# A state-space layer in one fused kernel: where the head's step sizes live, who makes its first taps, and the order of its last products

## The chip, the cores and the metric

The kernel runs on one core of one Trainium2 chip. The metric is the device time of one execution in microseconds. A core has TensorE (PE, matrix products into the PSUM banks), VectorE (DVE), ScalarE (ACT), GpSimd (POOL) and SyncE (SP), whose queue here issues nearly all DMAs. Engines run their own instruction streams and meet at counting semaphores.

## The reference, cut to what matters

Four layers over 512 tokens of width 1024: a short convolution with a feed-forward part, a dilated attention with a feed-forward part, a state-space mixer (SSD) and a gated linear attention mixer. Only the third is touched:

```python
def ssd_mixer(u, ...):                                   # u: rmsnorm(h), 512 x 1024
    z, xbc, dt = split(u @ w_in, [2048, 2048 + 4096])     # dt: 64 = 2 directions x 32 heads
    xbc = silu(dwconv(xbc, conv_w, conv_b))               # 5 taps along the tokens, per channel
    dt = softplus(dt + dt_bias); a = -exp(a_log)
    y = ssd_scan(xh, dt[:, :, 0], a[0], B, C) + rev(ssd_scan(rev(xh), rev(dt[:, :, 1]), a[1], rev(B), rev(C)))
    y = (y + xh * d_skip) * silu(z)                       # then an rmsnorm per group of 256 channels
    return y @ w_out
def step(state, (x, dt, la, B, C)):                       # one chunk of 128 tokens, la = dt * a
    cum = cumsum(la); decay = exp(cum_l - cum_s) where s <= l
    y = (C B^T * decay) @ (x * dt) + (C @ state) * exp(cum)
    state = state * exp(cum_end) + B^T @ (x * dt * exp(cum_end - cum))
```

All is fp32 to the reader. A matrix product is made of three products of fp32r parts: high with high, high with low, low with high.

## The kernel before, in words

**Weights** come in units of 128 x 2048 elements. SP loads a unit into `raw[s]` (s is the unit's parity), ScalarE copies it to its high part `whi[s]` (`high`, L684, line 690), GpSimd subtracts to get the low part `wlo[s]` (`low`, line 612). `high(n)` waits until TensorE has marked unit n-2 as done (semaphore `mm`, two marks a unit), SP's load of unit n until the low part of unit n-2 is made, and TensorE's `unit(n)` until the low part of n is there. So three engines work a unit or two ahead of TensorE, and a unit of 48 products of 512 columns takes TensorE some 11 us.

**The state-space stage** has 8 groups of 4 heads. For group g TensorE projects two x tiles, B and C (`project`, q = 0 to 3, channels on partitions, 512 tokens along the bank) and z. VectorE's `taps(g, q)` (L1528) scales the bank by the norm, makes the middle tap with a tensor_scalar (line 1536) and adds the four others (line 1540); ScalarE applies silu (`silu`, L905). TensorE turns x and B to tokens (`turn_x`, `turn_bc`), makes the scores B C^T (line 2273), which VectorE masks (line 1551), the state increments (line 2285), and for each of 4 chunks the carried and the intra-chunk products (lines 2317, 2321). The decay exp(cum_l - cum_s) is made from rows of cum that SP spreads over the partitions from DRAM: ScalarE biases them (`biased`, line 956), VectorE takes a minimum (`least`, line 1566), ScalarE the exponential (line 973). SP fetches the rows of chunk n only when the exponential of chunk n-2 is done. VectorE's `states` (L1568) runs the recurrence over chunks, `collect` (L1583) adds up a chunk: the carried products times exp(cum), into `yt`, the intra-chunk part, and then `yt` itself. `gate` multiplies by silu(z); `normalise`, with squares and a root on ScalarE, is the group norm; TensorE turns the result (line 2299), ScalarE keeps it and makes its high part (`y_hi`), VectorE its low part (`y_low`, line 1610).

**The head** has more: TensorE projects x, B, C of group 0, the step sizes dt (64 rows, bank 4) and x of group 1 one after the other. VectorE brings dt to SBUF and ScalarE and VectorE make softplus, dt * a, the cumulative sums (two scans, line 1687), cum_end - cum (line 1690), its exponential and the product with dt (line 1694), between the taps of group 0, in the written order of each engine.

**The tail.** The last group is written out by hand (`last_group`, on each engine). The output product has 8 units (128 output channels, 16 blocks of 128 inputs). Blocks 0 to 13 of units 0 and 1 are multiplied in while the last group still runs; blocks 14 and 15 belong to the last group and come last. The other units follow in a loop: all of a unit waits for its low part. When a unit's last product is marked, VectorE adds it to the residual (line 1328), and ScalarE makes the next norm's high part and square (`split_square`) and, behind these in its order, the high part of the weight unit two further on.

The order of every engine's work is written out; there is no planner.

## Time and profile before

| | us |
|---|---|
| median of 3 runs (lowest, highest) | 2104.53 (2103.15, 2105.02) |
| the profiled execution | 2103.18 |
| its span | 2101.2 |
| state-space stage, first projection to the last output unit | about 1168 to 1668 |

The page gives for each engine the busy time and its share of the span. The views name a wait by who waited and by the instruction that ended last before it could go on. Times in a timeline are microseconds from the start of the span. The stages before and after the state-space one have the same code before and after.

### The profile page before, as it was taken

How to read it: one execution, taken by the hardware profiler on the slowest of the kernel's cores; microseconds unless marked ns; L12 is line 12 of the kernel's file. 1: busy time of each engine (PE TensorE's matmuls, PEld its weight loads, DVE VectorE, ACT ScalarE, POOL GpSimd, SP SyncE). 2: the span in 40 equal slices, each digit the busy share in tenths (PEclk: the TensorE clock that was granted, in tenths of full speed). 3: DMA queues.
4: the chain of work that ended last, by engine and by line, in shares of the span. 5: the costliest groups of instructions: out<-in, count | busy, mean ns of one | idle time of the engine just before them, and what ended most of it. 6: DMA issues, size and time to landing. Idle time of an engine off the chain costs nothing.

```text
span 2101.2 us, 27300 instructions
## 1 busy us (share of the span) xinstructions
PE 2039.3 (97%) x10588; PEld 1698.2 (81%) x10588; DVE 930.4 (44%) x1425; ACT 838.0 (40%) x1349; POOL 1043.2 (50%) x855
## 2 busy tenths in 40 slices
PE   8999999999999999999999979999988999999998
PEld 6878888888777777888888768888976878888886
DVE  3184433421244443333313588888882224434231
ACT  4123222222344443222223467776772235553442
POOL 4445554545523324554455468888873432323342
PEclk9999999999999999999999989999998999999999
DMA  4223233323432213233233243443422331111231
GB/s 161 86 98 111 81 100 100 94 83 97 118 111 81 71 61 99 83 100 100 82 97 103 76 133 101 117 125 104 132 84 63 91 94 61 60 62 62 58 83 60
DMA packets 267034, 193.37 MB, mean 92 GB/s; under 512 B 9443, under 2 KB 263703, under 8 KB 266920
## 3 DMA queue, kind: packets, MB, share of 16 engines
q1 hardware_dynamic: 264380, 191.20, 30.6%
q8 instruction: 82, 1.34, 0.3%
q10 hardware_dynamic: 2540, 0.56, 0.1%
q14 instruction: 32, 0.26, 0.0%
HBM read 189.46 MB, written 2.27 MB: 91 GB/s over the span
## 4 chain that ended last, share of the span: by engine, by line
PE 54%; issue 24%; POOL 15%; DVE 4%; ACT 2%; DMA 0%; POOLq 0%; ACTq 0%; SPq 0%; DVEq 0%
PE bank L1895 16%; PE bank L1896 15%; PE bank L1897 15%; POOL wlo L612 15%; PE bank L2321 1%; PE bank L2504 1%; PE bank L2317 1%; PE bank L2285 1%; DVE xc L1540 1%; PE bank L2520 1%; ACT whi L690 0%; PE bank L2518 0%; PE bank L2478 0%; PE bank L2465 0%; DVE kg L1756 0%
## 5 line engine op out<-in xcount | busy, mean ns | idle before, releaser
L612 POOL TENSOR_TENSOR wlo<-raw,whi 128x512 fp32r<-128x512 f32 (+1 forms) x668 | 855.3, 1311 | 983.4 <-ACT whi L690 983.4
L1895 PE MATMUL bank<-hHi,whi 128*128 128x512 f32 x1408 | 557.1, 396 | 8.3 <-DVE xc L1540 2.9
L1897 PE MATMUL bank<-hHi,wlo 128*128 128x512 f32 x1408 | 549.1, 390 | 0.0
L1896 PE MATMUL bank<-hLo,whi 128*128 128x512 f32 x1408 | 548.8, 390 | 0.0
L690 ACT ACTIVATE whi<-raw 128x2048 fp32r<-128x2048 f32 (+1 forms) x168 | 303.7, 1808 | 456.3 <-PE bank L1897 451.7
L1895 PEld LDWEIGHTS bank<-hHi,whi 128*128 128x128 f32 x1408 | 264.8, 188 | 69.4 <-issue 8.5
L1897 PEld LDWEIGHTS bank<-hHi,wlo 128*128 128x128 f32 x1408 | 264.6, 188 | 56.2
L1896 PEld LDWEIGHTS bank<-hLo,whi 128*128 128x128 f32 x1408 | 264.9, 188 | 54.4 <-issue 1.2
L1895 PE MATMUL bank<-whi,hHi 128*128 128x256 f32 x896 | 262.8, 293 | 4.8 <-ACT gO L1205 3.7
L1897 PE MATMUL bank<-whi,hLo 128*128 128x256 f32 x896 | 253.4, 283 | 0.0
L1896 PE MATMUL bank<-wlo,hHi 128*128 128x256 f32 x896 | 253.3, 283 | 0.0
L1895 PEld LDWEIGHTS bank<-whi,hHi 128*128 128x128 f32 x896 | 171.6, 191 | 15.1 <-issue 14.7
L1896 PEld LDWEIGHTS bank<-wlo,hHi 128*128 128x128 f32 x896 | 171.6, 192 | 3.7 <-issue 3.7
L1328 DVE TENSOR_TENSOR xT<-xT,bank 128x512 f32<-128x512 f32 x48 | 33.0, 687 | 317.8 <-PE bank L1897 316.2
L1897 PEld LDWEIGHTS bank<-whi,hLo 128*128 128x128 f32 x896 | 171.5, 191 | 0.0
L1540 DVE SCALAR_TENSOR_TENSOR xc<-bank,vecT,xc 128x510 f32<-128x510 f32 (+1 forms) x96 | 72.0, 750 | 3.4
L1897 PE MATMUL bank<-f0aHi,wlo 128*128 128x512 f32 x176 | 68.5, 389 | 0.0
L1897 PE MATMUL bank<-f1aHi,wlo 128*128 128x512 f32 x176 | 68.5, 389 | 0.0
L1895 PE MATMUL bank<-f0aHi,whi 128*128 128x512 f32 x176 | 68.5, 389 | 0.0
L1896 PE MATMUL bank<-f0aLo,whi 128*128 128x512 f32 x176 | 68.5, 389 | 0.0
L1895 PE MATMUL bank<-f1aHi,whi 128*128 128x512 f32 x176 | 68.5, 389 | 0.0
L1896 PE MATMUL bank<-f1aLo,whi 128*128 128x512 f32 x176 | 68.5, 389 | 0.0
(340 smaller groups left out, 2923.3 us busy)
## 6 DMA issues: line engine op xcount, KB each, us to landing
raw<-in_ssd_w_in SPq DMA_DIRECT2D x48, 512.0 KB, 4.9
raw<-in_ffn_w_gate SPq DMA_DIRECT2D x44, 512.0 KB, 4.7
raw<-in_ffn_w_up SPq DMA_DIRECT2D x44, 512.0 KB, 4.6
raw<-in_gla_w_in SPq DMA_DIRECT2D x40, 512.0 KB, 4.5
rows<-cums SPq DMA_DIRECT2D x64, 256.0 KB, 5.5
raw<-in_conv_w_in SPq DMA_DIRECT2D x24, 512.0 KB, 4.4
raw<-in_ffn_w_down SPq DMA_DIRECT2D x32, 384.0 KB, 3.5
raw<-in_attn_w_qkv SPq DMA_DIRECT2D x24, 512.0 KB, 4.3
```

What stands on the lines that cost most here:

```text
L612: ins = pool.tensor_tensor(wlo[s][:, part], raw[s][:, part], whi[s][:, part].bitcast(F32), ALU.subtract)
L690: act.activation(whi[s][:, 0:w], raw[s][:, 0:w], ACT.Copy).then_inc(w_hi, 1)
L1328: tt(x, x, bank[b][:, :], ALU.add).then_inc(res_done, 1)
L1540: ins = stt3(y[:, to:to + w], u[:, frm:frm + w], tapcol(j, ct), y[:, to:to + w], ALU.mult, ALU.add)
L1895: pe.matmul(dst, hi1, hi2, start=first, stop=False)
L1896: pe.matmul(dst, hi1, lo2, start=False, stop=False)
L1897: return pe.matmul(dst, lo1, hi2, start=False, stop=last)
L2285: ins = pe.matmul(bank[4 + step][:, 256 * d:256 * d + 256], bt[:, P * c:P * (c + 1)], xw_buf(step, d), start=True, stop=True)
L2317: pe.matmul(carried_bank(c, d), conv_tile(g, 3)[:, P * c:P * (c + 1)], m["stt"][:, SEQ * step + 256 * d:SEQ * step + 256 * d + 256], start ...
L2321: ins = pe.matmul(intra_bank(c)[:, 64 * h:64 * h + 64], weights(n)[:, P * h:P * (h + 1)], xt[:, 256 * c + 64 * h:256 * c + 64 * h + 64], s ...
L2504: pe.matmul(bank[4 + 2 * d + n % 2][:, :], tile(t32[d], t, P), values(h, t), start=True, stop=True).then_inc(S("gu_mm"), 1)
L2520: ins = pe.matmul(out[:, :], decayed_q(h, d)[:, P * t:P * (t + 1)], state(d, t), start=n >= 2, stop=True)
```

## The change

Six edits:

1. Taps of group 0: VectorE scales the bank (`tap_scale`), ScalarE makes the middle tap out of the bank (`tap_mid`), VectorE adds the other four (`tap_rest`), with the four tiles interleaved. Groups 1 to 7 stay as they are.
2. The step sizes stay in PSUM bank 4 (`dt4`) through softplus and the later product; ScalarE makes a copy in SBUF for TensorE's transposes.
3. The end decays exp(cum_end - cum) are 8 ScalarE activations with scale -1 and a bias, one for each direction and chunk, in place of two VectorE subtractions and one exponential.
4. TensorE turns step sizes, sums and decays first and x of group 0 after them; ScalarE copies them in that order too.
5. `collect` writes the scaled carried product back to its bank and adds from there; `yt` goes, and the bank is released after the last add.
6. The last group on VectorE: `states` before the second `least`, `normalise` after two low parts; on TensorE: the last turn before the low parts of unit 1, unit 0 finished before unit 1's low weights, and unit 2 written out: 32 products with the high weights, which wait for the high part alone, then 16 with the low weights.

```diff
-                  ("stt", [P, 3 * SEQ], F32), ("xC1", V, F32), ("xt", [P, NT * 256], F32), ("MT", [P, 3 * SEQ], F32), ("yt", V, F32),
+                  ("stt", [P, 3 * SEQ], F32), ("xC1", V, F32), ("xt", [P, NT * 256], F32), ("MT", [P, 3 * SEQ], F32),
...
+    def tap_mid(g, q):
+
+        ct = 2 * g + q if q < 2 else (16 if q == 2 else 24) + g
+        act.wait_ge(S("tap_scaled"), 4 * g + q + 1)
+        act.activation(conv_tile(g, q), in_bank(g, q)[:, :], ACT.Copy, scale=tapcol(2, ct)).then_inc(S("tap_mid"), 1)
...
-    dtT, tmp, cum, wsT = headed("MT", 0), headed("MT", 1), headed("stt", 0), headed("stt", 2)
-    chain(act.activation(tmp, dtT, ACT.Abs, bias=hcol[:, 0:1]))
+    dt4, tmp, cum, wsT = bank[4][0:DTH, :], headed("MT", 1), headed("stt", 0), headed("stt", 2)
+    chain(act.activation(tmp, dt4, ACT.Abs, bias=hcol[:, 0:1]))
     chain(act.activation(tmp, tmp, ACT.Exp, scale=-1.0))
+    tap_mid(0, 0)
     act.activation(tmp, tmp, ACT.Ln, bias=1.0).then_inc(S("dt_log"), 1)
     unit_high(UNIT_OF["x", 1])
+    tap_mid(0, 1)
...
+    act.wait_ge(S("la_made"), 1)
+    copy(headed("MT", 0), dt4, S("dt_kept"))
     for q in range(2):
         silu(0, q)
+    tap_mid(0, 2)
     unit_high(UNIT_OF["bc", 1])
     act.wait_ge(S("cum_ready"), 1)
     for d in range(2):
         act.activation(dirs_of(m["hcol"][:, 4:8])[d].unsqueeze(2), last_of(cum, d), ACT.Exp).then_inc(S("decay_exp"), 1)
-    act.wait_ge(S("ws_diff"), 2)
-    act.activation(wsT, wsT, ACT.Exp).then_inc(S("decay_exp"), 1)
+    for d in range(2):
+        for c in range(NT):
+            ins = act.activation(v3(dirs_of(wsT)[d], NT)[:, c, :], v3(dirs_of(cum)[d], NT)[:, c, :], ACT.Exp, scale=-1.0,
+                                 bias=last_of(cum, d)[:, c, :])
+    ins.then_inc(S("decay_exp"), 1)
+    tap_mid(0, 3)
...
-    for b in range(2):
-        token_copy(0, b)
...
         copy(to, frm[:, ::-1, :] if d else frm, S("decay_kept"))
+    for b in range(2):
+        token_copy(0, b)
     silu(0, 2)
...
-    tt(dtT, bank[4][0:DTH, :], rstd[0:DTH, :], ALU.mult).then_inc(S("dt_pre"), 1)
+    dt4 = bank[4][0:DTH, :]
+    tt(dt4, dt4, rstd[0:DTH, :], ALU.mult).then_inc(S("dt_pre"), 1)
...
         chain(tt(u[:, :], u[:, :], rstd[:, :], ALU.mult))
         chain(ts(y, u[:, :], tapcol(2, ct), None, ALU.mult))
+        taps_beside(g, q)
+
+    def taps_beside(g, q):
+
+        ct = 2 * g + q if q < 2 else (16 if q == 2 else 24) + g
...
         ins.then_inc(S("tap_done"), 1)
+
+    def tap_scale(g, q):
+
+        dve.wait_ge(mm, 2 * UNIT_OF["x" if q < 2 else "bc", g] + q % 2 + 1)
+        u = in_bank(g, q)
+        tt(u[:, :], u[:, :], rstd[:, :], ALU.mult).then_inc(S("tap_scaled"), 1)
+
+    def tap_rest(g, q):
+
+        dve.wait_ge(S("tap_mid"), 4 * g + q + 1)
+        taps_beside(g, q)
...
-        y, yt = chunk("ybuf", c), m["yt"]
...
+        y = chunk("ybuf", c)
...
         dirs = [d for d in range(2) if not (c == 0 and d == 0) and not (c == 3 and d == 1)]
         if len(dirs) == 2:
-            chain.note(tt(dh(yt[:, :]), dh(bank[(5, 7)[c - 1]][:, :]), heads2("ecum", c, g), ALU.mult))
+            carried = bank[(5, 7)[c - 1]][:, :]
+            chain.note(tt(dh(carried), dh(carried), heads2("ecum", c, g), ALU.mult))
         else:
-            d = dirs[0]
-            chain.note(tt(h4(yt[:, 256 * d:256 * d + 256]), h4(carried_bank(c, d)), bc(heads("ecum", c, d, g), 64), ALU.mult))
+            carried = carried_bank(c, dirs[0])
+            chain.note(tt(h4(carried), h4(carried), bc(heads("ecum", c, dirs[0], g), 64), ALU.mult))
         chain(tt(y, y, intra_bank(c), ALU.add))
+        for n in range(len(dirs)):
+            chain(tt(y, y, carried[:, 256 * n:256 * n + 256], ALU.add))
         dve.sem_inc(S("y_bank_free"), 1)
-        for d in dirs:
-            chain(tt(y, y, yt[:, 256 * d:256 * d + 256], ALU.add))
...
         normalise(g - 1)
         least(n)
         low(U_SSD_OUT)
+        states(g)
         least(n + 1)
-        states(g)
         y_low(0)
         least(n + 2)
         for k in range(1, 3):
@@ -1638,10 +1671,10 @@
         collect(g, 2)
         collect(g, 3)
         gate(g, 1)
-        for k in range(5, 10):
+        for k in range(5, 7):
             y_low(k)
         normalise(g)
-        for k in range(10, IT):
+        for k in range(7, IT):
             y_low(k)
...
-    taps(0, 0)
+    tap_scale(0, 0)
+    tap_scale(0, 1)
+    tap_rest(0, 0)
     dve.wait_ge(S("dt_log"), 1)
-    chain(ts(dtT, dtT, hcol[:, 0:1], 0.0, ALU.add, ALU.max))
-    chain(tt(dtT, dtT, tmp, ALU.add))
+    chain(ts(dt4, dt4, hcol[:, 0:1], 0.0, ALU.add, ALU.max))
+    tt(dt4, dt4, tmp, ALU.add).then_inc(S("dt_made"), 1)
+    dve.wait_ge(S("dt_made"), 1)
     dve.wait_ge(S("decay_exp"), 1)
-    chain(ts(laT, dtT, hcol[:, 1:2], -1.0, ALU.mult, ALU.mult))
-    taps(0, 1)
+    ts(laT, dt4, hcol[:, 1:2], -1.0, ALU.mult, ALU.mult).then_inc(S("la_made"), 1)
+    dve.wait_ge(S("la_made"), 1)
+    tap_rest(0, 1)
+    tap_scale(0, 2)
     for d in range(2):
         way = slice(None, None, -1 if d else 1)
         chain(dve.tensor_tensor_scan(dirs_of(cum)[d][:, way], dirs_of(again)[d], dirs_of(laT)[d][:, way], 0.0, ALU.mult, ALU.add))
     dve.sem_inc(S("cum_ready"), 1)
-    for d in range(2):
-        tt(v3(dirs_of(wsT)[d], NT), last_of(cum, d).broadcast_to([SSD_HEADS, NT, P]), v3(dirs_of(cum)[d], NT), ALU.subtract).then_inc(S("ws_diff"), 1)
+    tap_scale(0, 3)
+    tap_rest(0, 2)
     dve.wait_ge(S("decay_exp"), 3)
     tt(v3(m["back"][0:DTH, 0:256], NT), rep(ident[0:DTH, 0:DTH], NT), bc(m["hcol"][0:DTH, 4:8], DTH), ALU.mult).then_inc(S("et_spread"), 1)
     dve.wait_ge(S("decay_exp"), 4)
-    tt(wsT, wsT, dtT, ALU.mult).then_inc(S("ws_made"), 1)
-    for q in range(2, 4):
-        taps(0, q)
+    tt(wsT, wsT, dt4, ALU.mult).then_inc(S("ws_made"), 1)
+    tap_rest(0, 3)
...
-            pe.wait_ge(S("dt_pre"), 1)
+            pe.wait_ge(S("dt_kept"), 1)
+            pe.wait_ge(S("ws_made"), 1)
...
         out_high(1, range(14))
-        out_low(1, range(14))
         for e in range(2):
             turn_out(g, e)
-        unit(U_SSD_OUT + 1)
-        out_low_weight(1, range(14))
+        out_low(1, range(14))
         for k in range(2):
+            if k:
+                unit(U_SSD_OUT + 1)
+                out_low_weight(1, range(14))
             for j in range(14, IT):
                 out_high(k, (j,))
                 out_low_weight(k, (j,))
                 mark(out_low(k, (j,)))
 
-    turn_x(0)
     pe.wait_ge(S("cum_ready"), 1)
+    pe.wait_ge(S("dt_kept"), 1)
...
+    turn_x(0)
...
-    for k in range(2, KT):
+    pe.wait_ge(w_hi, U_SSD_OUT + 3)
+    for j in range(IT):
+        w = slice(P * j, P * (j + 1))
+        pe.matmul(out_bank(2)[:, :], whi[0][:, w], tile(sHi, j), start=j == 0, stop=False)
+        pe.matmul(out_bank(2)[:, :], whi[0][:, w], tile(sLo, j), start=False, stop=False)
+    unit(U_SSD_OUT + 2)
+    for j in range(IT):
+        ins = pe.matmul(out_bank(2)[:, :], wlo[0][:, P * j:P * (j + 1)], tile(sHi, j), start=False, stop=j == IT - 1)
+        if j >= IT - 2:
+            mark(ins)
+    for k in range(3, KT):
```

## Rows read from the trace of the kernel before

**Rows 1.** The page's first part: engine, busy us (share of the span), instructions.

```profile
PE 2039.3 (97%) x10588; PEld 1698.2 (81%) x10588; DVE 930.4 (44%) x1425; ACT 838.0 (40%) x1349; POOL 1043.2 (50%) x855
```

**Rows 2.** TensorE's waits, whole span: waited for; us in total, times, longest.

```profile
PE bank L1895 <- POOL wlo L612: 11.8, 4, 8.5
...
PE bank L2317 <- DVE stt L1580: 5.5, 2, 3.3
...
PE bank L2273 <- ACT xC L908: 3.1, 1, 3.1
PE bank L2266 <- ACT xc L908: 2.9, 1, 2.9
PE bank L1895 <- DVE xc L1540: 2.9, 1, 2.9
```

**Rows 3.** Two stretches: busy us of each engine, granted clock, DMA share, GB/s.

```profile
1280.00:1325.00 45.00, 45.00 (x277) 40.24 (x276) 38.97 (x56) 31.42 (x69) 38.51 (x34) 1.00 0.44 118
1601.00:1605.00 4.00, 3.28 (x9) 2.61 (x10) 0.00 (x0) 0.00 (x0) 4.00 (x4) 0.55 0.48 138
```

**Rows 4.** Timeline of VectorE, head: start, us, line, operation, tile, count, idle before.

```profile
1191.67 0.47 DVE L1680 TENSOR_SCALAR MT<-MT,hcol 64x512 f32<-64x512 f32 x1
1192.17 1.66 DVE L1681 TENSOR_TENSOR MT<-MT 64x512 f32<-64x512 f32 x1
...
1202.45 2.38 DVE L1690 TENSOR_TENSOR stt<-stt 32x512 f32<-32x512 f32 x2 [0.15 <-DVE stt L1687]
...
1213.92 3.10 DVE L1540 SCALAR_TENSOR_TENSOR xC<-bank,vecT,xC 128x510 f32<-128x510 f32 x4
...
1217.66 0.75 DVE L1536 TENSOR_SCALAR xc<-bank,vecT 128x512 f32<-128x512 f32 x1
...
1221.47 0.68 DVE L1551 TENSOR_TENSOR CB<-bank,LE 128x512 f32<-128x512 f32 x1
```

**Rows 5.** Groups of instructions by line: count, busy us, mean ns, idle before.

```profile
L1599 DVE TENSOR_TENSOR ybuf<-ybuf,yt 128x256 f32<-128x256 f32 x48 | 42.7, 889 | 5.5 <-DVE ybuf L1596 4.9
...
L1596 DVE TENSOR_TENSOR ybuf<-ybuf,bank 128x256 f32<-128x256 f32 x32 | 13.1, 409 | 0.0
...
L956 ACT ACTIVATE rows<-rows,ncum 128x128 f32<-128x128 f32 x128 | 40.7, 392 | 8.5 <-DMA rows<-cums 8.3
...
L999 ACT ACTIVATE sY<-bank,vecT 128x512 f32<-128x512 f32 x16 | 10.7, 671 | 12.2 <-PE bank L2299 12.2
```

**Rows 6.** Timeline of TensorE, head.

```profile
1208.74 1.03 PE L2257 MATMUL bank<-ident,xc 128*128 128x128 f32 x8
...
1217.83 2.08 PE L2273 MATMUL bank<-xC,xc 128*128 128x128 f32 x8 [3.11 <-ACT xC L908]
```

**Rows 7.** Timeline of ScalarE, head.

```profile
1209.38 1.08 ACT L710 ACTIVATE xt<-bank 128x512 f32<-128x512 f32 x2 [3.88 <-PE bank L2257]
...
1213.23 0.72 ACT L908 ACTIVATE xc<-xc,vecT 128x512 f32<-128x512 f32 x1
```

**Rows 8.** Timelines of the last group and the tail: VectorE, TensorE, ScalarE, GpSimd.

```profile
1540.72 2.67 DVE L1617 TENSOR_TENSOR wlo<-raw,whi 128x2048 fp32r<-128x2048 f32 x1 [1.33 <-ACT whi L690]
1547.01 0.70 DVE L1566 TENSOR_TENSOR bank<-bank,rows 128x512 f32<-128x512 f32 x1 [3.61 <-ACT bank L956]
...
1592.00 0.69 DVE L1328 TENSOR_TENSOR xT<-xT,bank 128x512 f32<-128x512 f32 x1 [1.68 <-PE bank L2361]
...
1561.25 1.13 PE L2317 MATMUL bank<-stt,xC 128*128 128x256 f32 x4 [1.93 <-ACT szs L981]
...
1587.10 3.43 PE L2355 MATMUL bank<-sHi,wlo 128*128 128x512 f32 x14
...
1601.72 0.80 PE L1895 MATMUL bank<-sHi,whi 128*128 128x512 f32 x1 [8.47 <-POOL wlo L612]
...
1593.87 1.89 ACT L690 ACTIVATE whi<-raw 128x2048 fp32r<-128x2048 f32 x1
...
1595.84 10.78 POOL L612 TENSOR_TENSOR wlo<-raw,whi 128x512 fp32r<-128x512 f32 x8 [24.42 <-ACT whi L690]
```

More of the change, by code:

```diff
@@ L1521, in _ @@
                 dve.wait_ge(S("rstd_ready"), MID + 1)
-                dtT, tmp, laT, cum, wsT = headed("MT", 0), headed("MT", 1), headed("MT", 2), headed("stt", 0), headed("stt", 2)
+                tmp, laT, cum, wsT = headed("MT", 1), headed("MT", 2), headed("stt", 0), headed("stt", 2)
                 hcol = m["hcol"][0:DTH, :]
-                tt(dtT, bank[4][0:DTH, :], rstd[0:DTH, :], ALU.mult).then_inc(S("dt_pre"), 1)
+                dt4 = bank[4][0:DTH, :]
+                tt(dt4, dt4, rstd[0:DTH, :], ALU.mult).then_inc(S("dt_pre"), 1)
                 dve.wait_ge(S("spread"), MID + 1)
@@ L1531, in taps @@
                     y = conv_tile(g, q)
-                    n = 4 * g + q
                     dve.wait_ge(mm, 2 * UNIT_OF["x" if q < 2 else "bc", g] + q % 2 + 1)
@@ L1536, in taps @@
                     chain(ts(y, u[:, :], tapcol(2, ct), None, ALU.mult))
+                    taps_beside(g, q)
+                def taps_beside(g, q):
+                    ct = 2 * g + q if q < 2 else (16 if q == 2 else 24) + g
+                    y, u = conv_tile(g, q), in_bank(g, q)
                     for j in (0, 1, 3, 4):
```

## The prediction

> **What bounds the kernel now.** The page first: TensorE is busy for 97% of the span [rows 1], so an edit on another engine can pay only where TensorE stands idle, or runs at the lower clock after it has. The next view, what TensorE waited for over the whole execution [rows 2], names those places. One wait of 8.5 us for a low weight half made on GpSimd is the largest in the kernel; it lies at the end of the state-space stage. The head of that stage has four: 3.1 and 2.9 us for a ScalarE silu, 2.2 us (with the 3.3 us of the last group in one row) for the states, 2.9 us for VectorE's taps. In the last group TensorE also waits 1.9 us for the silu of z [rows 8]. The stretches [rows 3] show the rest: in a middle group TensorE is busy for 45.00 of 45 us, so whatever VectorE saves there is hidden, and after the long wait the granted clock is 0.55, near the lower of the two levels.
>
> All of the change therefore has to be read at two places, 1185 to 1240 us and 1545 to 1605 us. At the head VectorE works almost without a break from 1186 us on: it ends tap (0,3) at 1217.0 (its row starts at 1213.92 and takes 3.1), tap (1,0) at 1221.5, and then masks the scores [rows 4].
>
> **Head: taps and decays.** Each of the four tiles loses one VectorE tensor_scalar (0.78 us with its gap) to ScalarE, where the nearest row is a scaled copy out of PSUM, 671 ns [rows 5]; VectorE gains 3.1 us. The step sizes stay in bank 4. The SBUF-with-SBUF add took 1.66 us beside GpSimd's weight halves [rows 4]; with one operand in PSUM the adds of this kernel take 0.69 at 512 columns, as the first mask row does with 0.68. That is 1.0 us, and I take as much again for the last product, which has the same form. The two subtractions for the end decays (2.38 us in all, same form [rows 4]) go away. Against it stand the first tensor_scalar, which alone took 0.47 us and with PSUM takes 0.75, and nothing else on VectorE. Sum for VectorE: 3.1 + 1.0 + 1.0 + 2.4 + 0.4 (the product with a_log, which also sat beside GpSimd) - 0.3 = 7.6 us earlier at the end of tap (0,3), at about 1209.4.
>
> One rule speaks against the move to PSUM. The 0.47 us row is an SBUF tensor_scalar, the 0.75 us row one from PSUM [rows 4]. The Trainium skill (VectorE: DVE Perf Modes, "Why PSUM operands drop a tier") says that a PSUM operand costs such an instruction its double rate, and the trace agrees. By that rule alone two tensor_scalars would lose 0.3 us each; the row with GpSimd at work gives the second one back, as it was slowed more than that.
>
> ScalarE takes on 8 exponentials in place of 1: pieces of 128 columns start 0.31 us apart (392 ns each in the row, with overlap) [rows 5], 2.5 us for 0.6; four middle taps, 2.7 us; and one copy of the step sizes, 0.6. It stood idle for 3.9 us before 1209.38 [rows 7] and for longer before silu (0,1), which holds all of it, except that the first middle tap stands ahead of the high weight half of the next x unit. That moves this half by 0.65 us; its low half on GpSimd then no longer runs beside VectorE's slow add, and I cost this at nothing (if not, TensorE waits 0.65 us longer for that unit).
>
> Not all of the 7.6 us arrives. TensorE reaches its transposes at 1208.74 whatever VectorE does [rows 6]: its projections fill the time until then. Then comes a chain that the change leaves as long as it is: small transposes (1.4 us, now ahead of turn_x), five ScalarE copies and two token copies (2.6 from the first to the table load), the load (1.28) and silu (0,2) (0.72): it ends at 1214.0, where before it ended at 1213.95 [rows 7]. TensorE's turn of it and the copy take until 1215.4, silu (0,3) until 1216.1. Only this last one waited for VectorE, whose tap ended at 1217.0, and TensorE's scores came at 1217.83 [rows 6]. Scores now start at 1216.1 and, at the lower clock as before, are there about 2 us later. VectorE has done tap (1,0) by 1215.7 and waits; the first mask starts at 1218.2 against 1221.47, that is 3.3 us earlier. Everything behind it (least, exponential, row DMAs, states, chunk 0, tap (1,1)) keeps its distance, so project (1,3), which starts at 1236.03 when tap (1,1) has ended (the 2.9 us wait), starts at 1232.7. From there TensorE was full. **Head: -3.3 us**, bounds -1 (the ScalarE chain eats most) and -5.8 (1221.5 less 1215.7, if it were VectorE alone).
>
> **Collects.** 48 adds of 889 ns (SBUF with SBUF, beside GpSimd) become adds of 409 ns from PSUM [rows 5]: 23 us of VectorE work, of it some 20 in middle groups, hidden under a full TensorE. The bank is released after the last add, 0.9 us later; the next x transposes that wait for it came 5.6 us after the old release at group 0. Nothing for both. In the last group the collects end about 2 us sooner, which the next part uses up.
>
> **Last group: states ahead of the second minimum.** states starts at 1543.4, when VectorE has made its weight half, not behind the second minimum at 1547.6 [rows 8], and so ends about 4 us sooner, at 1548.0 by its five pieces (4.6 us). TensorE's 3.3 us wait goes. But the second minimum, at 1547.01, slips by 1.0 us. The exponential, the DMA of the last decay rows, their biases, the last exponential and silu z follow one after another, and TensorE's wait for z moves from 1561.25 [rows 8] to 1562.25 and grows from 1.9 to some 7.5 us. The wait of 1.9 us left the clock alone, that of 8.5 us did not: in the 4 us behind it 9 matmuls start at a clock of 0.55, 0.43 us apart, where 14 at the full clock take 3.43 us [rows 3, 8], 1.3 us lost. I expect the same here. (The Trainium skill, TensorE: Matmul & The Clock Gate, Part 1, says the throttled state is the default and activity releases it; these rows agree, and by the row alone the loss is the same.) So 2.3 us are lost there and the 2 us from collects come back. normalise now stands after two low parts instead of five. VectorE's total is unchanged and ScalarE's root covers itself as before, so the 14th low part still comes when it did, and TensorE waits as long for the parts, only elsewhere. Net +0.4, bounds -2 and +2.
>
> **Tail: output unit 2.** The last matmul of units 0 and 1 starts at 1592.86 and the next at 1601.72, 8.47 us of idle time [rows 8]. In between: the first residual (1592.00), ScalarE's split and square, the high half (1593.87, 1.89 us), GpSimd's low half (5.4 of the 10.78 us for two). The new loop needs only the high half for its first 32 matmuls, 32 x 0.227 = 7.3 us, which covers the 5.4. And the turns and unit 0's end now come before unit 1's 14 low-weight products (3.43 us at 1587.10) and 6 others (1.4). From the first residual, which follows unit 0's last matmul by 0.5 us, to the end of the high half are 1595.76 - 1592.00 = 3.8 us, so 4.3 in all; TensorE has 4.8 us of work. So the gap closes, with 0.5 us to spare: -8.5. The clock isn't lost either: -1.3. Of what moves: unit 0's end now stands behind the same four ScalarE and two VectorE pieces (4.0 us from the first turn) with 14 low products (3.2) and the turns (0.8) as cover: nothing. GpSimd makes the halves of units 2 and 3 back to back, 10.8 us from the end of the high half; TensorE wants unit 3 after 0.5 + 10.9: it just fits. SP's loads of units 2 and 3 wait for halves of units 0 and 1 alone, which GpSimd ended 24 us before its next work, and are long there. **Tail: -9.8 + 0.4 = -9.4 us**, bounds -12 and -6.
>
> **Sum.** -3.3 - 9.4 = -12.7 us. Against the profiled execution (2103.18 us, span 2101.2) that is 2090.5; the median of the runs, 2104.53, stands 1.35 above it, and the prediction goes by it: 2091.8. Changes within 0.2% (4 us) can't be told from none here.
>
> **Rivals.** (a) Only the tail pays: ScalarE, with the added pieces between, brings silu (0,2) and (0,3) no earlier. For it: the chain above has no slack to 1214.0. Against: 9 us of idle time on ScalarE. 2104.5 - 9.4 = 2095.1. (b) Both in full: the scores come when VectorE is ready, z is not later and the collects' 2 us count: -5.8 - 9.8 - 2.0 = -17.6, 2086.9. Against: the rows DMA follows the exponential. (c) Unit 2 doesn't close the gap: if ScalarE's order or the load holds back the high half as long as before, only the low half (5.4 us) is covered; 2104.5 - 3.3 - 5.4 = 2095.8, or 2099 with the head lost as well. (d) Slower: the collects now write their product back into its bank and read it there once or twice more, while TensorE fills others; no row shows a head-broadcast product from PSUM into PSUM. If they held the banks longer, TensorE would stall at the x transposes in each of 7 groups. The release has 5.6 us of room, of which 0.9 is used; the kernel is slower than before only if each release comes 4.7 + 12.7/7 = 6.5 us later still. VectorE has only 6 us of idle time per group, so that would cost as much: at 7.5 us later, 7 x 2.8 - 12.7 = +7, 2111.
>
> **Chances.** Forecast 60%, (a) 13%, (b) 10%, (c) 12%, (d) 2%, nothing or less by other causes 3%. Faster by over 0.2%: 93%; within: 4%; slower: 3%. The range takes in (a), (b) nearly, and (c): 2086.5 to 2098.
>
> **What would show it.** Head: "TensorE waits for ScalarE xC" at about 1216, the first mask at 1218.2, project (1,3) at 1232.7; VectorE idle before the mask by 2 to 3 us (it had none). Middle groups: TensorE still 45 of 45, VectorE's adds at 0.41. Last group: no wait for the states, one of about 7 us for silu z, then 0.5 of the clock. Tail: no wait of over 1 us between the last matmul of unit 1 and unit 2. It is wrong if the wait for z is short, if the gap before unit 2 stays, or if a middle group is longer than 45 us.

## The result, and the profile after

The kernel after takes **2090.97 us** (median of 5 runs, 2089.01 to 2092.32), the kernel before on the same chip 2103.15 (5 runs, 2101.06 to 2105.02): 12.2 us less. The ratio is 0.9939, 95% interval 0.9926 to 0.9951; by the ratio it is 12.8 us less, with an interval of 10.3 to 15.6. Forecast were 2091.8 us and -12.7, counted from the median of 2104.53 that was known then. The profiled execution took 2089.12 us (span 2087.4), against 2103.18 (2101.2) before.

To read where the time went, the span is cut at four instructions that every version has: the first scale of the step sizes on VectorE, the start of project(1, 3) on TensorE, VectorE's first mask of the last group, and the first residual of output unit 2 (the third `xT<-xT,bank` of 128x512). Times in us, each from one profiled execution:

```
kernel                                 first cut   head  middle  last group+tail   rest    span
before                                   1185.94  50.09  298.83      79.40       486.94  2101.2
after                                    1183.23  46.82  298.91      71.45       486.99  2087.4
the tail edit alone                      1186.09  50.10  299.14      69.44       486.93  2091.7
after, states behind the least gates     1184.60  47.27  299.34      69.15       487.04  2087.4
after, TensorE's wait for z filled       1185.86  47.27  298.78      69.48       487.11  2088.5
after, unit 2 as before                  1183.63  47.31  298.85      79.01       487.00  2095.8
after, taps on VectorE                   1183.67  46.54  299.16      71.70       488.33  2089.4
after, step sizes in SBUF                1186.36  47.29  300.02      70.27       486.96  2090.9
after, silu table early                  1184.17  44.46  299.08      71.42       486.97  2086.1
after, collects through SBUF             1185.69  46.81  298.87      72.13       487.00  2090.5
after, table early + states behind       1185.72  44.71  299.71      69.39       486.97  2086.5
the same, wait filled                    1184.20  45.86  299.47      69.26       487.01  2085.8
after, again                             1183.13  47.26  298.79      71.51       486.91  2087.6
```

The pair of executions differs by 13.8 us: 3.3 in the head, 8.0 in the last group and tail, nothing in the middle, and 2.7 ahead of the first cut, where both kernels are the same. That last part is a difference between executions (the column holds 1183.1 to 1186.4 for kernels that don't differ there). 1.6 us of it arise at one place: behind a wait of 1.8 us that both kernels have, the granted clock from 794 to 798 us is 0.80 in before and 1.00 in after. So the change is worth 11.2 us by the two stretches of the pair, 12.2 by the medians and 12.8 by the ratio. Where the code of a stretch is the same, the column scatters too: by 0.5 us in the head (by 1.4 in the three kernels with the early table), 1.2 in the middle and 1.4 in the last stretch; single numbers are read with that in mind. The rest column holds 486.9 to 487.1 but for one execution of 488.33; there the granted clock is 0.61 from 1708 to 1712 us, where the kernel after has 1.00.

The page's first part answers to [rows 1]. VectorE has lost 34 us, of which the kernel got little: TensorE is what counts.

```profile
PE 2035.4 (98%) x10588; PEld 1695.2 (81%) x10588; DVE 896.1 (43%) x1419; ACT 843.0 (40%) x1361; POOL 1034.3 (50%) x855
```

What TensorE waited for, whole span, against [rows 2]:

```profile
PE bank L2355 <- ACT szs L996: 6.3, 1, 6.3
...
PE bank L1932 <- POOL wlo L612: 3.3, 3, 1.8
PE bank L1932 <- DVE xc L1561: 3.1, 1, 3.1
PE bank L2304 <- ACT xc L908: 2.9, 1, 2.9
...
PE bank L2399 <- DVE sLo L1643: 2.4, 1, 2.4
...
PE bank L2355 <- DVE stt L1612: 1.3, 1, 1.3
...
PE bank L2311 <- ACT xC L908: 1.3, 1, 1.3
```

The 8.5 us for a low weight half are gone, the wait for the states fell from 5.5 (2.2 in the head, 3.3 in the last group) to the 1.3 of the head, and the one for silu (0, 3) from 3.1 to 1.3. New is 6.3 us for the silu of z, and 2.4 for a low part of y.

A middle stretch, against [rows 3], and the groups of the collects, against [rows 5]. TensorE is as full as it was; VectorE has 36.0 us of work in 45 instead of 39.0.

```profile
1280.00:1325.00 45.00, 45.00 (x276) 40.22 (x275) 36.01 (x56) 31.66 (x68) 37.59 (x35) 1.00 0.44 118
```

```profile
L1631 DVE TENSOR_TENSOR ybuf<-ybuf,bank 128x256 f32<-128x256 f32 x48 | 20.2, 421 | 1.7
...
L1629 DVE TENSOR_TENSOR ybuf<-ybuf,bank 128x256 f32<-128x256 f32 x32 | 13.1, 408 | 0.0
```

The head on VectorE, after, against [rows 4] (times in this and the following fences are of an execution whose head starts 2.71 us earlier than that of before):

```profile
1202.70 3.11 DVE L1561 SCALAR_TENSOR_TENSOR xC<-bank,vecT,xC 128x510 f32<-128x510 f32 x4
1208.58 0.70 DVE L1550 TENSOR_TENSOR bank<-bank,rstd 128x512 f32<-128x512 f32 x1 [2.77 <-PE bank L2295]
...
1215.47 0.69 DVE L1583 TENSOR_TENSOR CB<-bank,LE 128x512 f32<-128x512 f32 x1 [2.27 <-PE bank L2311]
```

The taps of (0, 3) end at 1205.8, 8.5 us sooner than before after alignment; VectorE then stands idle twice. TensorE and ScalarE there, against [rows 6, 7]:

```profile
1211.43 0.63 PE L2304 MATMUL bank<-ident,xc 128*128 128x128 f32 x4 [2.89 <-ACT xc L908]
1213.36 2.08 PE L2311 MATMUL bank<-xC,xc 128*128 128x128 f32 x8 [1.29 <-ACT xC L908]
```

```profile
1206.81 0.38 ACT L710 ACTIVATE dt<-bank 128x256 f32<-128x256 f32 x1 [4.15 <-PE bank L2275]
...
1209.27 1.28 ACT L908 ACT_TABLE_LOAD   x1
1210.57 0.72 ACT L908 ACTIVATE xc<-xc,vecT 128x512 f32<-128x512 f32 x1
```

The last group and the tail, against [rows 8]: TensorE, then GpSimd.

```profile
1555.42 2.08 PE L2355 MATMUL bank<-stt,xC 128*128 128x256 f32 x4 [6.28 <-ACT szs L996]
1557.29 1.81 PE L2359 MATMUL bank<-xt,MT 128*128 128x64 f32 x8
...
1570.10 4.41 PE L2399 MATMUL bank<-sLo,whi 128*128 128x512 f32 x7 [2.41 <-DVE sLo L1643]
1574.31 5.20 PE L2388 MATMUL bank<-sHi,whi 128*128 128x512 f32 x14
...
1589.10 0.39 PE L2399 MATMUL bank<-sLo,whi 128*128 128x512 f32 x1
1589.33 0.39 PE L2459 MATMUL bank<-sHi,whi 128*128 128x512 f32 x1
...
1600.21 0.39 PE L1932 MATMUL bank<-sHi,whi 128*128 128x512 f32 x1
```

```profile
1588.92 10.95 POOL L612 TENSOR_TENSOR wlo<-raw,whi 128x512 fp32r<-128x512 f32 x8 [24.30 <-ACT whi L690]
```

Unit 2 follows unit 1 at the pace of the matmuls (1589.10, 1589.33), and unit 3 starts at 1600.21, 0.34 us after GpSimd's last low half ends at 1599.87. Behind the 6.28 us wait four state products take 2.08 us where they took 1.13 [rows 8]: the granted clock is 0.50 there (rows in the last section).

### The profile page after: what moved, and what is told of

The parts are those of the page before. It is cut to its first block, busy times and chain, and to the rows that moved or that the text cites. A ratio compares the mean times of both kernels' runs of the same rounds, so it can differ in the third digit from the quotient of the medians.

```text
span 2087.4 us, 27284 instructions
## 1 busy us (share of the span) xinstructions
PE 2035.4 (98%) x10588; PEld 1695.2 (81%) x10588; DVE 896.1 (43%) x1419; ACT 843.0 (40%) x1361; POOL 1034.3 (50%) x855
## 3 DMA queue, kind: packets, MB, share of 16 engines
HBM read 189.46 MB, written 2.27 MB: 92 GB/s over the span
## 4 chain that ended last, share of the span: by engine, by line
PE 56%; issue 23%; POOL 15%; DVE 3%; ACT 2%; DMA 0%; POOLq 0%; ACTq 0%; SPq 0%; DVEq 0%
PE bank L1932 16%; PE bank L1934 15%; PE bank L1933 15%; POOL wlo L612 15%; PE bank L2359 1%; PE bank L2554 1%; PE bank L2355 1%; PE bank L2323 1%; PE bank L2570 1%; ACT whi L690 0%; PE bank L2568 0%; PE bank L2399 0%; PE bank L2528 0%; PE bank L2515 0%; PE bank L2311 0%
```

## Experiments

Every kernel named "after, ..." above is the kernel after with one edit. Numbers of experiments 1 to 8 are of one profiled execution each; 9 to 11 are timed over five runs.

**1. The tail edit alone**, put on the kernel before.

```
-                    out_low(1, range(14))
                     for e in range(2):
                         turn_out(g, e)
-                    unit(U_SSD_OUT + 1)
-                    out_low_weight(1, range(14))
+                    out_low(1, range(14))
                     for k in range(2):
+                        if k:
+                            unit(U_SSD_OUT + 1)
+                            out_low_weight(1, range(14))
...
+                pe.wait_ge(w_hi, U_SSD_OUT + 3)
+                for j in range(IT):
+                    w = slice(P * j, P * (j + 1))
+                    pe.matmul(out_bank(2)[:, :], whi[0][:, w], tile(sHi, j), start=j == 0, stop=False)
+                    pe.matmul(out_bank(2)[:, :], whi[0][:, w], tile(sLo, j), start=False, stop=False)
+                unit(U_SSD_OUT + 2)
...
```

> The kernel before with TensorE's tail alone changed: last turns ahead of unit 1's low parts, unit 0 finished before unit 1's low weights, unit 2 written out behind its high half. Measured by the tail distance, from the first mask of the last group on VectorE to the first residual of unit 2: 79.4 us before (1534.86 to 1614.26), 71.45 after (1528.96 to 1600.41). Theory A (the tail edit is worth all of its 8.6 us of idle time and 1.5 us of slow clock, and the other edits of the last group cost 2.2 us of it by a longer wait at a low clock): 79.4 - 10.1 = 69.3, that is shorter than in the full change. Theory B (the tail edit itself falls short by 2 us, the last group's edits are free): 71.4 or more. The head distance (step sizes scaled to project (1,3)) stays at 50.1.

Measured: head 50.10, last stretch 69.44, time 2093.54 us. The edit is worth 10.0 us by itself (79.40 to 69.44), as theory A has it, and the rest of the change makes this stretch 2.0 us longer.

**2. States behind the second least gates again.**

```
                     low(U_SSD_OUT)
-                    states(g)
                     least(n + 1)
+                    states(g)
```

> The changed kernel with VectorE's states of the last group behind the second minimum again. Theory A: TensorE waits 3.3 us before chunk 0 and some 2 us for silu z in place of 6.3 us for z; the slow clock then falls on chunks 0 and 1, which end before z anyway, and chunk 2 and its followers run at the full one: tail distance 69.2 (71.45 - 2.2). Theory B (states early is worth its 3.3 us, the slow clock costs nothing): 73 or more. Neither: 71.4.

Measured: 69.15, 2.3 us shorter than after (71.45, and 71.51 in its second profile). TensorE waits more often and less long:

```profile
1548.92 0.70 PE L2355 MATMUL bank<-stt,xC 128*128 128x256 f32 x2 [3.32 <-DVE stt L1612]
...
1557.52 1.13 PE L2355 MATMUL bank<-stt,xC 128*128 128x256 f32 x4 [1.75 <-ACT szs L996]
1558.49 1.00 PE L2359 MATMUL bank<-xt,MT 128*128 128x64 f32 x8
```

Counted from the first mask of the group (1528.96 after, 1531.21 here), the wait for z ends at 26.46 us after and 26.31 here; chunk 3 is done 34.3 and 31.5 us behind it. So states early saves 3.3 us of waiting for the states and gives it all back at the next wait, since z comes when it came; only the clock differs behind it. The move is a loss: the five executions with this tail and the states early have 70.27 to 71.70 (mean 71.3), the two with the states behind 69.15 and 69.39 (experiment 9), 2.0 us less on the mean.

**3. TensorE's wait for z filled** with output products that needed neither chunk 2 nor 3.

```
-                    for ks in (range(0, 4), range(4, 6)):
+                    for ks in (range(0, 4), range(4, 5)):
...
-                        if ks.start == 0:
-                            chunk_out(g, 2)
-                    out_low(0, range(0, 4))
+                    out_low(0, range(0, 3))
+                    for j in range(5, 8):
+                        out_high(0, (j,))
+                        out_low_weight(0, (j,))
+                    out_low(0, range(3, 5))
+                    chunk_out(g, 2)
                     chunk_out(g, 3)
```

> The changed kernel with the 6.3 us wait for z filled: TensorE makes unit 0's high, low-weight and low products of blocks 0 to 7 as far as they are ready before chunk 2, and chunk 3 follows chunk 2 at once. Nothing is left out. Theory A (that wait and the clock after it set the tail): no wait of over 1.5 us there, a clock of 0.9 or more at chunk 2, chunk 3 done some 4 us sooner, VectorE's normalise and low parts with it: tail distance 66.5, between 66 and 68. Theory B (VectorE's own work between the collects and the 14th low part sets it): 70 to 71.

Measured: 69.48, which neither theory gave; it is nearer to the 70 of theory B than to the 66.5 of theory A. The wait for z shrank to 0.2 us and both chunks ran at the full clock, done 30.6 us behind the first mask, 3.8 sooner than after. Little of it arrived, for VectorE was then late (its timeline, this kernel):

```profile
1564.72 1.72 DVE L1638 TENSOR_TENSOR szs<-szs,ybuf 128x512 f32<-128x512 f32 x1 [0.15 <-DVE ybuf L1631]
1566.37 3.44 DVE L1643 TENSOR_TENSOR sLo<-sY,sHi 128x512 fp32r<-128x512 f32 x2
...
1571.51 4.30 DVE L1643 TENSOR_TENSOR sLo<-sY,sHi 128x512 fp32r<-128x512 f32 x7
```

The gate took 1.72 us and a low part 1.7, against 0.69 for the gate in the kernel after: in this kernel GpSimd made its weight half from 1563.38 to 1569.3, beside them, there from 1559.59 to 1564.6. TensorE waited 5.5 us for low parts and 2.5 for high ones. The Trainium skill (SBUF — State Buffer, "Who interferes with whom") says that a VectorE instruction with two SBUF inputs contends with a GpSimd instruction that reads SBUF; the trace agrees. Not every such instruction pays: in experiment 2 the same gate took 0.73 us beside the same weight half, and there it was GpSimd's piece beside it that took 1.7 us instead of 1.2.

**4. Output unit 2 in the loop as before**, the reordered tail kept.

```
-                pe.wait_ge(w_hi, U_SSD_OUT + 3)
...
-                for k in range(3, KT):
+                for k in range(2, KT):
                     unit(U_SSD_OUT + k)
```

> The changed kernel with unit 2 back in the loop, so that it waits for its low half as in the kernel before; the reordered tail stays. Theory A (the written-out unit is the edit that closes the gap): GpSimd's 5.4 us are seen again, less 0.5 of slack, and 1.3 us of slow clock: tail distance 71.45 + 6.2 = 77.7. Theory B (the reorder of units 0 and 1 closes it alone): 71.5 to 73.

Measured: 79.01, time 2097.51; theory A, but 1.3 us more than its 77.7. The wait comes back (the row below), and the slow clock with it: nine matmuls take 4.0 us from start to start, where they take 2.0 at the full pace.

```profile
1595.70 0.80 PE L1932 MATMUL bank<-sHi,whi 128*128 128x512 f32 x1 [5.34 <-POOL wlo L612]
```

So 7.6 of the 10 us hang on needing only the high half (5.3 of wait, 2.0 of clock). The rest is put down to the reorder ahead of it by subtraction; the reorder was not run alone on the kernel before.

**5. Group 0's taps all on VectorE**, end decays and step sizes as after.

```
-                tap_mid(0, 0)
...
-                tap_scale(0, 0)
-                tap_scale(0, 1)
-                tap_rest(0, 0)
+                taps(0, 0)
...
```

> The changed kernel with the four taps of group 0 wholly on VectorE again; step sizes in PSUM, end decays on ScalarE stay. Measured by the head distance, from the scaling of the step sizes on VectorE to the start of project (1,3) on TensorE: 50.09 us before, 46.82 after. Theory A (the chain TensorE turns, ScalarE copies, table load, two silus sets the head, VectorE waits 2.8 us before tap (1,0) and 2.3 us before the mask): VectorE is 3.1 us later, all of it in these waits: 46.8 to 47.2. Theory B (VectorE still sets it): 46.8 + 3.1 = 49.9.

Measured: head 46.54, not longer than after. VectorE reaches tap (1, 0) 3.1 us later than after, where it then stood waiting, so it starts it without a wait at 1209.32; the mask still waits:

```profile
1215.64 0.69 DVE L1579 TENSOR_TENSOR CB<-bank,LE 128x512 f32<-128x512 f32 x1 [1.70 <-PE bank L2303]
```

The kernel after has this wait of TensorE, for the low weight half of the next x unit:

```profile
1194.94 0.50 PE L1932 MATMUL bank<-hHi,whi 128*128 128x512 f32 x1 [0.65 <-POOL wlo L612]
```

It is gone here, because no middle tap stands ahead of the high half on ScalarE: GpSimd starts the low half 5.90 us behind the first cut in place of 6.61, and TensorE reaches the small transposes at 22.10 in place of 22.83. The slower taps cost nothing elsewhere in the head: against the second profile of the kernel after (47.26), where the turn of B and the scores ran at the same slow clock as here, the head is 0.7 us shorter. So the taps on ScalarE bought nothing once the other edits were in, and cost 0.7 us, as far as one execution shows.

**6. Step sizes in SBUF and the end decays on VectorE as before**, the taps kept on ScalarE.

```
-                dt4 = bank[4][0:DTH, :]
-                tt(dt4, dt4, rstd[0:DTH, :], ALU.mult).then_inc(S("dt_pre"), 1)
+                tt(dtT, bank[4][0:DTH, :], rstd[0:DTH, :], ALU.mult).then_inc(S("dt_pre"), 1)
...
+                tt(..., last_of(cum, d)..., ALU.subtract).then_inc(S("ws_diff"), 1)
```

> The changed kernel with the step sizes in SBUF and the end decays by two VectorE subtractions and one exponential, as before; the first taps on ScalarE stay. Theory A as for the taps: VectorE is 4.5 us later, of which its waits take 4 or more, and the product with dt ends some 0.5 us too late for TensorE's small transposes: head distance 47 to 48. Theory B (the slow SBUF adds were what set the head): 51.

Measured: head 47.29, close to the kernel after (46.82, 47.26); theory A's range. VectorE waits 0.88 us ahead of tap (1, 0) and 2.27 ahead of the mask. It reaches tap (1, 0) 2.4 us later than after and not 4.5, since the add and the product of the step sizes, both SBUF with SBUF, took 0.68 us each and not the 1.66 and 1.77 of the kernel before. The add:

```profile
1192.74 0.68 DVE L1710 TENSOR_TENSOR MT<-MT 64x512 f32<-64x512 f32 x1
```

GpSimd's weight half starts at 1193.01 here, after this add has started, and at 1191.86 in the kernel before, ahead of its add at 1192.17; the product starts behind the next half here, and beside it there. So the 1 us each that the move to PSUM was to bring was the price of what ran beside these instructions. TensorE's wait for the low half is 1.14 us in this kernel, 0.5 more than after.

Either half of VectorE's relief alone gives a head of 46.5 to 47.3 against 50.1. Both kernels keep the new order of TensorE's transposes (edit 4); what that does alone was not run.

**7. The silu table asked for early**, in ScalarE's idle time.

```
+                act.activation(stat[:, 63:64], ident[:, 0:1], ACT.Silu)
                 act.wait_ge(S("dt_turned"), 2)
```

> The changed kernel with one more ScalarE instruction, a silu of one column into an unused place, ahead of the copies of the step sizes, where ScalarE stands idle for 4.2 us: the table load of silu (0,2) then lies in that idle time. Theory A (ScalarE's chain sets the head): silus, scores and mask come 1.3 us sooner, head distance 45.5. Theory B (VectorE or the row DMAs set it): 46.8.

Measured: head 44.46, 2.4 us shorter, time 2087.87. ScalarE and TensorE in this kernel:

```profile
1203.62 1.28 ACT L1099 ACT_TABLE_LOAD   x1
...
1209.08 1.11 ACT L710 ACTIVATE xt<-bank 128x512 f32<-128x512 f32 x2
1210.04 0.75 ACT L908 ACTIVATE xc<-xc,vecT 128x512 f32<-128x512 f32 x1
```

```profile
1210.93 0.63 PE L2305 MATMUL bank<-ident,xc 128*128 128x128 f32 x4 [1.46 <-ACT xc L908]
1212.85 1.16 PE L2312 MATMUL bank<-xC,xc 128*128 128x128 f32 x8 [1.30 <-ACT xC L908]
```

The load of 1.28 us lies in idle time, silu (0, 2) follows the copies at once, and TensorE's wait is 1.5 us instead of 2.9; it starts its turn of B 1.4 us sooner. The eight score products then take 1.16 us and not 2.08: the clock stayed up, another 0.9. Together that is the 2.4, but only the 1.4 come each time (experiments 9 and 10). It is ScalarE's chain that sets the head; with it shortened, VectorE goes from tap (1, 0) to the mask without a wait, so here the two end together.

**8. Collects through an SBUF tile**, as before.

```
-                        carried = bank[(5, 7)[c - 1]][:, :]
-                        chain.note(tt(dh(carried), dh(carried), heads2("ecum", c, g), ALU.mult))
+                        chain.note(tt(dh(yt[:, :]), dh(bank[(5, 7)[c - 1]][:, :]), heads2("ecum", c, g), ALU.mult))
...
```

> The changed kernel with collect as before, through the SBUF tile yt. Theory A (the collects lie under a full TensorE in groups 0 to 6, and in the last group under its waits for chunks 2 and 3): head distance 46.8, the middle from project (1,3) to the first mask of the last group 298.9 as in both kernels, tail distance 71.5 to 72. Theory B (VectorE's 23 us count): the middle 2 us or more longer, the tail 73.5.

Measured: middle 298.87 (298.91 after), last stretch 72.13 (71.45, 71.51). 23 us of VectorE work are worth nothing in the middle, and 0.7 us in the last group, which is inside the scatter of 1.4. TensorE's wait for z ends 27.21 us behind the first mask, 0.75 later than after.

**9 to 11. The best of it, timed.** Edits 7 and 2 together; the same with edit 3; and the kernel after again, all on one chip.

> The kernel after with two edits that were each profiled alone: the silu table asked for while ScalarE waits for the turned step sizes, and the second half of the least gates of each chunk ahead of the states again. Theory A (the two act in stretches that don't touch): head 44.5, last group and unit 2 69.2, the middle and the rest as before; the time is then the kernel after less 2.4 and less 2.3, about 2086.3, a ratio to the kernel before of 0.992. Rival B (the last group's gain was the scatter of one execution): head 44.5, last stretch 70.5 to 71.7, about 2088. Rival C (TensorE's clock gives either back later): no better than the kernel after, 2090 to 2091.

> The same two edits, and TensorE's order of the last group in which its wait for z's last rows is filled with the output projection's products before the last two chunks. Theory A (states early had made VectorE late there; with the gates ahead of them the chunks are done sooner, and the fill keeps the clock up): last stretch 67 to 68.5, time about 2085. Rival B (VectorE's gates and splits beside GpSimd's weight half are what the fill then waits for, with or without the states): last stretch 69 to 70.5, time 2086 to 2087.5, no better than without the fill.

> The kernel after itself, on the same chip as the two versions above, so that they are compared with it and not over two jobs. Every theory: a ratio to the kernel before of 0.993 to 0.995, head 46.8 to 47.3, last stretch 70.3 to 71.7.

Measured, with 2101.86 us for the kernel before (9 runs, 2100.3 to 2105.69):

```
                              median   5 runs                ratio to before, 95% interval
table early + states behind   2087.60  2085.90 to 2088.55    0.9927 [0.9913, 0.9941]
the same, wait filled         2087.50  2086.11 to 2088.46    0.9929 [0.9915, 0.9942]
after, again                  2090.29  2089.06 to 2094.98    0.9947 [0.9933, 0.9960]
```

The first is 2.7 us faster than the kernel after: its slowest run lies below the fastest of that, though the intervals to the kernel before overlap. The two stretches of its profiled execution came as expected (44.71 and 69.39), 2.6 and 2.1 us shorter than in the kernel after again, yet the medians differ by 2.7 and not by 4.7.

One part of that is the middle, 299.71 against 298.79. There the 3.1 us wait ahead of project(1, 3) is followed by the slow clock in every kernel: the matmuls start 0.43 us apart instead of 0.23, for 3.3 us in the kernel after and for 5.1 here. This doesn't show rival C, though. Experiment 2, whose code is that of the kernel after up to the last group, has 4.2 us (middle 299.34), and experiment 6, with neither of the two edits, 5.9 us (middle 300.02). The length differs between executions, and nothing here shows that the edits make it longer.

The other part is the head. The kernel with the filled wait has the same head and took 45.86 us for it, since its scores ran at the slow clock:

```profile
1213.36 2.08 PE L2312 MATMUL bank<-xC,xc 128*128 128x128 f32 x8 [1.30 <-ACT xC L908]
```

They took 1.41 us in the first kernel of the table and 1.16 in experiment 7. The early table is worth 1.4 us at the same clock (47.26 to 45.86) and up to 2.4 where the clock stays up. The filled wait adds nothing (rival B): TensorE waits 4.3 us for low parts in place of 3.1.

## Why the prediction was right, step by step

**Head, -3.3 predicted, -2.8 to -3.3 measured.** The head took 50.09 and 50.10 us before. Six executions have the code of the kernel after there: two took 46.8 and four 47.3, by whether the turn of B took 0.63 us or 1.09 at the slow clock. That the profiled one gave the forecast number is luck; the mechanism is shown. Aligned to before's start of the head, taps (0, 3) end at 1208.5 (predicted 1209.4, so VectorE gained 8.5 us and not 7.6), the scores start at 1216.1 (1216.1), the mask at 1218.2 (1218.2) and project(1, 3) at 1232.8 (1232.7). The step that carried it, "only silu (0, 3) waited for VectorE", was tested from both sides: half of VectorE's gain loses little or nothing (5, 6), and 1.3 us on ScalarE's chain gives 1.4 to 2.4 (7, 9, 10). The upper bound of 5.8, VectorE alone, was never in reach. The product and add of the step sizes take 0.68 and 0.69 us from PSUM, as costed, but from SBUF they took 0.68 as well once GpSimd's weight half no longer came first (6). The first middle tap ahead of the high weight half was put at nothing, and against the kernel before it is nothing (TensorE waits 0.65 us for the low half, 0.71 before): the half starts 0.7 us later and takes 5.04 us in place of 5.79. Without that tap the wait goes away (5).

**Collects, 0 predicted in the middle, 0 measured** (8). Rival (d), held banks, is out: the product written back to its bank takes 0.69 us at 512 columns, as it did into SBUF. But the 2.0 us that the collects were to give in the last group came as 0.3 to 0.7, which the scatter covers: the tail edit alone, with the old collects and the old place of normalise, has 69.44, the kernel that differs from after only in the states' place 69.15, and collects through SBUF add 0.7 to after (8). What VectorE saves there ahead of z's arrival is saved while TensorE waits for ScalarE; that this is the reason is argued and not tested, and it isn't the whole of it, since in 8 z came 0.75 us later.

**States ahead of the gates, +2.3 predicted, +2.3 measured** (2; +2.0 by the means), but of other parts. z was to come 1.0 us later and came 0.15 later: the second least gates slipped 0.5, and ScalarE waits 0.77 us for the decay rows of the last chunk, but it no longer waits 0.75 us for the third gates. TensorE's wait for z was to be 7.5 us and is 6.3. The clock was to cost 1.3 and cost 2.7 on chunks 2 and 3 (they are done 34.33 us behind the first mask and 31.45 in 2, less the 0.15); I had sized it by the nine matmuls behind another wait [rows 3]. VectorE's low parts made up for 1.8 of it (the last of unit 0 is done 45.55 us behind the first mask, 44.56 before), but unit 1's 14 high products behind the wait of 2.4 us for them take 5.20 us at a slow clock, where they took 4.07.

So the term of the sum that was mis-sized is the **last group's net: +0.4 predicted, +2.1 measured** (unit 1's high products end that much later behind the first mask, 50.39 us against 48.27), because the collects' 2.0 us did not come back. The fault was to count a gain of VectorE where TensorE was waiting for ScalarE, which the prediction had avoided in the head and the middle.

**Tail, -9.8 predicted, -10.0 measured** (1). The high half is ready 0.48 us before unit 2 starts (predicted 0.5), the low half of unit 3 0.34 us before it is wanted, and no clock is lost. That refutes rival (c), by which the high half would have been late. Experiment 4 shows what the low half would have cost, a wait of 5.34 us where 5.4 was forecast.

**Sum.** By the stretches -3.3 - 8.0 = -11.3, against -12.7; by the medians -12.2, by the ratio -12.8. What the timed runs have over the stretches lies within what separates two executions of the same code (2.7 us ahead of the first cut in the profiled pair). So the agreement of the ratio to 0.1 us is luck: by the stretches the forecast gain was 1.4 us too large, and the last group's term accounts for it.

## What to carry to other kernels

A product that needs only the half of its operand that is ready first can run while the other half is made: the new order of TensorE's last products was worth 10 us, 7.6 of them by this rule, and nothing else in the change came near it. Ahead of moving work from a busy engine, look for the chain that TensorE waits for: 34 us taken from VectorE gave 3 us, and one instruction that put a table load into ScalarE's idle time gave 1.4 to 2.4. Two short waits of TensorE can be cheaper than one long one (3.3 and 1.8 us against 6.3 here), since the slow clock then falls on work that has time. And a gain of under 1.5 us in one execution means little here until the granted clock of both executions is laid beside it.

## What was not expected of the hardware

- The slow stretch behind a wait is not of one length or price, even for the same code. Behind the wait ahead of project(1, 3), 3.12 us in all kernels but before (2.88), it lasted from 3.2 to 5.9 us in the thirteen executions; behind the 1.8 us wait near 792 us it was there in six of them and not in seven. After 6.28 us of waiting the granted clock was 0.50, the lower of the two levels (1.2 GHz), from 1555.5 to 1560.5 (rows below, the kernel after) and chunks 2 and 3 together took 2.7 us longer. Behind the 1.93 us wait of before [rows 8] the clock cost nothing.

```profile
1555.50:1557.00 1.50, 1.50 (x4) 1.23 (x5) 1.31 (x3) 1.50 (x4) 1.21 (x1) 0.50 0.00 0
1557.00:1560.50 3.50, 3.50 (x14) 3.12 (x13) 1.59 (x4) 3.50 (x6) 0.91 (x1) 0.50 0.00 0
1560.50:1563.20 2.70, 2.70 (x16) 2.31 (x16) 0.53 (x2) 1.41 (x5) 2.70 (x3) 0.88 0.00 0
```

- A table load cost ScalarE 1.28 us and nothing more: in the kernel after silu (0, 2) starts 1.30 us behind the start of the load (1209.27, 1210.57). The Trainium skill (ScalarE: Activation LUTs, "What ACT_TABLE_LOAD costs") gives 2.66 us for a switch, a drain included. The rows show the load alone, and the measurement decides; an estimate from the page's figure would have put the early table 1.4 us too high.
